# Routing in a two-layer diffusion kernel: seats of the first round from the prefix sums, gate work split, ranked weights behind the first gathers' index

## The reference

```python
aff = jax.nn.sigmoid((t @ router_w).astype(jnp.float32))
sel = aff + router_b.astype(jnp.float32)
...
_, idx = lax.top_k(jnp.where(in_group, sel, -jnp.inf), TOP_K)
wsel = jnp.take_along_axis(aff, idx, axis=-1)
wsel = wsel / jnp.sum(wsel, axis=-1, keepdims=True)
gates = jnp.sum(jax.nn.one_hot(idx, N_EXPERTS, dtype=jnp.float32) * wsel[..., None], axis=1)
a = jnp.einsum('nd,edf->nef', t, w1)
b = jnp.einsum('nd,edf->nef', t, w3)
hid = jax.nn.silu(a) * b * gates[..., None].astype(t.dtype)
return jnp.einsum('nef,efd->nd', hid, w2).reshape(B, L, D)
```

## Time and profile before

| what | value |
|---|---|
| median of 3 runs | 1009.19 us (1008.07 to 1012.16) |
| the profiled execution, its own time | 1012.8 us |
| its span, first to last instruction | 1010.7 us |
| PE busy | 896.8 us (89%) |
| DVE, ACT, POOL busy | 493.1 (49%), 250.9 (25%), 178.3 (18%) us |
| mean granted TensorE clock | 0.945 of full speed |
| moved by DMA | 213.74 MB |

### The profile page before, as it was taken

How to read it: one execution, slowest core, us unless ns; L and a number is a source line. 1 busy time by engine, 2 the same in 40 slices (tenths; PEclk the granted TensorE clock), 3 DMA queues, 4 the chain that set the end, 5 groups by cost and what they waited for, 6 DMA issues and landing times.

```text
span 1010.7 us, 12292 instructions
## 1 busy us (share of the span) xinstructions
PE 896.8 (89%) x4293; PEld 514.3 (51%) x4293; DVE 493.1 (49%) x1167; ACT 250.9 (25%) x606; POOL 178.3 (18%) x214
## 2 busy tenths in 40 slices
PE   2999989989979998969998989999998599689778
PEld 0685455655456544724443448747654463533223
DVE  1215763676879335533332371376577772422124
ACT  2202213535545112301111021221446240311000
POOL 1625220211000000320121101612112000121100
PEclk8899999999989998979998999999999799599899
DMA  9887222485700102778997591923584018869993
GB/s 373 264 240 222 83 84 84 170 317 209 290 16 2 42 0 89 284 284 295 387 420 304 207 339 76 252 83 97 182 320 153 0 57 323 328 232 398 418 400 136
DMA packets 69650, 213.74 MB, mean 211 GB/s; under 512 B 9690, under 2 KB 18178, under 8 KB 60372
## 3 DMA queue, kind: packets, MB, share of 16 engines
q1 hardware_dynamic: 58912, 187.81, 49.5%
q0 software_dynamic: 9504, 21.88, 6.9%
q10 hardware_dynamic: 1172, 3.24, 0.8%
HBM read 198.95 MB, written 21.31 MB: 218 GB/s over the span
## 4 chain that ended last, share of the span: by engine, by line
PE 74%; DVE 12%; issue 5%; DMA 4%; ACT 2%; POOL 2%; SPq 0%; DVEq 0%; ACTq 0%; POOLq 0%
PE bank L2014 14%; PE bank L1924 8%; PE bank L1720 8%; PE bank L1616 8%; PE bank L2038 7%; PE bank L1696 4%; PE bank L1870 3%; PE bank L1708 3%; PE bank L1803 3%; PE bank L1663 3%; DMA BRANCH<-in_w_mod 3%; PE bank L1891 2%; POOL ST L1249 2%; PE bank L1779 2%; PE bank L2071 1%
## 5 line engine op out<-in xcount | busy, mean ns | idle before, releaser
L2014 PE MATMUL bank<-RINGW,NA 128*64 128x512 f32 (+1 forms) x400 | 140.7, 619 | 20.6 <-issue 15.8
L1249 POOL TENSOR_TENSOR ST<-ST,RT 128x1 f32<-128x1 f32 (+4 forms) x46 | 52.0, 1132 | 409.7 <-DVE ST L2184 224.2
L1720 PE MATMUL bank<-RINGW,H 128*128 128x512 f32 (+4 forms) x384 | 120.7, 476 | 0.0
L2014 PEld LDWEIGHTS bank<-RINGW,NA 128*64 128x64 f32 (+1 forms) x400 | 51.3, 157 | 99.4 <-issue 99.4
L1720 PEld LDWEIGHTS bank<-RINGW,H 128*128 128x128 f32 x384 | 69.7, 193 | 49.1 <-issue 44.6
L1924 PE MATMUL bank<-RINGW,H 128*128 128x512 f32 x192 | 84.9, 603 | 0.1
L2801 DVE SCALAR_TENSOR_TENSOR BRANCH<-BRANCH,bank 128x256 f32<-128x256 f32 x20 | 8.4, 421 | 137.1 <-ACT BRANCH L1586 79.2
L1616 PE MATMUL bank<-IDENT,BRANCH 128*128 128x128 f32 (+1 forms) x271 | 40.9, 299 | 26.0 <-DVE BRANCH L2475 12.4
L1586 ACT ACTIVATE BRANCH<-bank 128x256 f32<-128x256 f32 x20 | 7.7, 384 | 214.0 <-PE bank L2014 214.0
L1924 PEld LDWEIGHTS bank<-RINGW,H 128*128 128x128 f32 x192 | 36.8, 193 | 45.4 <-issue 45.4
L1616 PEld LDWEIGHTS bank<-IDENT,BRANCH 128*128 128x128 f32 (+1 forms) x271 | 33.0, 148 | 45.7 <-issue 22.9
(11 more groups left out here) (354 smaller groups left out, 1525.9 us busy)
## 6 DMA issues: line engine op xcount, KB each, us to landing
RINGW<-in_moe_w SPq DMA_DIRECT2D x50, 1024.0 KB, 11.3
RINGW<-in_w_mod SPq DMA_DIRECT2D x23, 2048.0 KB, 8.2
WORK<-in_moe_w SPq DMA_DIRECT2D x14, 1024.0 KB, 12.8
W2R<-in_moe_w SPq DMA_DIRECT2D x12, 1024.0 KB, 12.3
PROJ<-in_moe_w SPq DMA_DIRECT2D x10, 1024.0 KB, 9.5
RINGW<-in_w_out SPq DMA_DIRECT2D x4, 2048.0 KB, 9.2
RINGW<-in_w_in SPq DMA_DIRECT2D x4, 1536.0 KB, 15.8
pairs<-NA POOLq DMA_DIRECT2D x12, 512.0 KB, 9.7
```

What stands on the lines that cost most here:

```text
L1249: pool.tensor_tensor(r[:, 0:w], m[:, 0:w], POOL_HALF[:, 0:w], ALU.pow).then_inc(rstd_ready, 1)
L1720: ins = pe.matmul(bank_of(s)[:, 0:nn], HT[:, kk, t * P:(t + 1) * P], wv[:, kk, off:off + nn], start=kk == 0, stop=kk == KD - 1)
L2014: ins = pe.matmul(bank_of(s)[seats, :], XGT[n % 2][:, kk, seats], w[:, kk, :], start=kk == 0, stop=kk == KD - 1)
```

## The change

- `sel` is made in one operation from the half-scaled tanh and a prepared bias (`BIASH`); `aff` is made behind `ASSIGN`.
- In `pfx`, DVE first makes the seats of round 0 straight from the prefix sums and the `SEND` rows from them (`IOTA` now counts from 1); the step `oh` is gone. Layer 0 needs one operation for the seats, layer 1 three.
- The gate work is split: up to the reciprocal it stays in `rT`, the other six operations stand in `pfx` behind `SEND` and ahead of `pick`.
- The list: `gdiff` goes ahead of `slots`, `gsel 0` goes behind `ab 0`.
- SP's load of the first ranked weights also waits for `index_ready`.

```diff
@@ make_schedule
-            if t == 3 and 0 in sq:
-                s += [("oh", l, 0)]
...
-        s += [("pfx", l, 1), ("oh", l, 1), ("gbc2", l)]
+        s += [("pfx", l, 1), ("gbc2", l)]
         s += [("xT", l, 0), ("tot", l)] if early else [("tot", l), ("xT", l, 0)]
-        s += [("slots", l), ("xg", l, 1), ("xg", l, 2), ("gdiff", l), ("gsel", l, 0), ("ab", l, 0)]
+        s += [("gdiff", l), ("slots", l), ("xg", l, 1), ("xg", l, 2), ("ab", l, 0), ("gsel", l, 0)]
@@ SP
                         sp.wait_ge(*full_of(("xT", p[1], 0, 1)))
                         sp.wait_ge(h2_stored, 16 * T)
+                        sp.wait_ge(index_ready, 1)
@@ DVE, gates
+                        link(dve.tensor_scalar(BIASH, bc_rb, 0.5, None, ALU.add))
@@ DVE, rT
-                    link(dve.tensor_scalar(aff, RT[:, 320 + 32 * s[2]:352 + 32 * s[2]], 0.5, 0.5, ALU.mult, ALU.add))
...
-                    link(dve.tensor_tensor(s3, a3, bc_rb.unsqueeze(1).broadcast_to([P, nt, 16]), ALU.add))
+                    half = RT[:, 320 + 32 * s[2]:352 + 32 * s[2]]
+                    link(dve.scalar_tensor_tensor(s3, half.rearrange("p (t e) -> p t e", e=16), 0.5,
+                                                  BIASH.unsqueeze(1).broadcast_to([P, nt, 16]), ALU.mult, ALU.add))
...
                     dve.wait_ge(assign_ready, pfx_n[("pfx",) + s[1:]])
+                    link(dve.tensor_scalar(aff, half, 0.5, 0.5, ALU.mult, ALU.add))
                     link(dve.tensor_tensor(gt, of_tiles(ASSIGN, t0), a3, ALU.mult))
                     link(dve.tensor_reduce(mx, gt, AX.X, ALU.add))
                     link(dve.reciprocal(mx, mx))
-                    link(dve.tensor_scalar(mx, mx, 0.5, None, ALU.mult))
-                    gv = GATEv[:, t0:t0 + 2, :]
-                    link(dve.tensor_tensor(gv, gt, bcast(mx, 16), ALU.mult))
-                    for c, oh in ((0, oh0), (1, oh1)):
-                        link(dve.tensor_tensor(prod, oh, gv, ALU.mult))
-                        link(dve.tensor_reduce(ENT[:, t0:t0 + 2, c, 1], prod, AX.X, ALU.add))
@@ DVE, pfx
                     bk = bank_of(s)
+                    pos, mine = of_tiles(bk, 0), of_tiles(ASSIGN, t0)
+                    sent_to = [SEAT[:, 2 * i:2 * i + 2] for i in (0, 1)]
+                    if l < DEPTH - 1:
+                        link(dve.tensor_tensor(sent_to[0], pos[:, :, 0], mine[:, :, 0], ALU.mult))
+                    else:
+                        half = N_E // 2
+                        dve.tensor_tensor(sent_to[0], pos[:, :, 0], mine[:, :, 0], ALU.mult)
+                        link(dve.scalar_tensor_tensor(sent_to[1], pos[:, :, half], float(P // 2), mine[:, :, half],
+                                                      ALU.add, ALU.mult))
+                        link(dve.tensor_tensor(sent_to[0], sent_to[0], sent_to[1], ALU.add))
+                    for i in (0, 1):
+                        ins = dve.tensor_scalar(SEND[0][t0 + i], IOTA[:, :], SEAT[:, i:i + 1], None, ALU.is_equal)
+                    ins.then_inc(send_ready, 1)
+                    mx = RT[:, 240:242]
+                    gt, prod = of_tiles(RT[:, 280:], 0), of_tiles(PROD, 0)
+                    link(dve.tensor_scalar(mx, mx, 0.5, None, ALU.mult))
+                    gv = GATEv[:, t0:t0 + 2, :]
+                    link(dve.tensor_tensor(gv, gt, bcast(mx, 16), ALU.mult))
+                    for c in (0, 1):
+                        link(dve.tensor_tensor(prod, of_tiles(OH[c], t0), gv, ALU.mult))
+                        link(dve.tensor_reduce(ENT[:, t0:t0 + 2, c, 1], prod, AX.X, ALU.add))
@@ DVE, iota
-                    dve.tensor_copy(IOTA[:, :], bank_of(s)[:, 0:P]).then_inc(iota_ready, 1)
+                    dve.tensor_scalar(IOTA[:, :], bank_of(s)[:, 0:P], 1.0, None, ALU.add).then_inc(iota_ready, 1)
@@ DVE, oh: the whole step is removed
-                        link(dve.tensor_scalar(SEAT[:, 2 * T * r + 2 * t0:2 * T * r + 2 * t0 + 4],
-                                               SLOTF[:, 2 * t0:2 * t0 + 4], -float(r), 1.0 / nr, ALU.add, ALU.mult))
...
-                            ins = dve.tensor_scalar(SEND[r][t], IOTA[:, :], seat(r, t, 0), None, ALU.is_equal)
...
-                            ins = dve.scalar_tensor_tensor(SEND[r][t], IOTA[:, :], seat(r, t, 1), SEND[r][t],
-                                                           ALU.is_equal, ALU.add)
```

More of the change, by code:

```diff
@@ L637, in build @@
         NOTOVER = ST[:, 250:251]
-        SEAT = ST[:, 136:136 + DIRECT * 2 * T]
+        SEAT = ST[:, 136:140]
+        BIASH = ST[:, 160:176]
         RSEAT = ST[:, 144:144 + 2 * 2 * T]
@@ L2740, in _ @@
                     tick(dve, free_of(s)[0])
[L2741 to L2746, removed]
-                        link(dve.tensor_scalar(SEAT[:, 2 * T * r + 2 * t0:2 * T * r + 2 * t0 + 4],
-                                               SLOTF[:, 2 * t0:2 * t0 + 4], -float(r), 1.0 / nr, ALU.add, ALU.mult))
-                    for r in range(DIRECT):
-                        for t in (t0, t0 + 1):
-                            ins = dve.tensor_scalar(SEND[r][t], IOTA[:, :], seat(r, t, 0), None, ALU.is_equal)
-                        link(ins)
-                        for t in (t0, t0 + 1):
-                            ins = dve.scalar_tensor_tensor(SEND[r][t], IOTA[:, :], seat(r, t, 1), SEND[r][t],
-                                                           ALU.is_equal, ALU.add)
-                        ins.then_inc(send_ready, 1)
                 elif k == "slots":
```

## The result

The changed kernel takes 1014.96 us in the median of 8 runs (1012.58 to 1018.19), the kernel before 1009.93 in the median of 8. The ratio is 1.0054 (95% interval 1.0034 to 1.0074): **5 us slower**. The forecast was 1006.3, with 999.5 to 1011 as the range. Of all runs in this document one, in the last experiment, was slow (1180 us, at a granted clock of 0.756); it is left out.

The account below looks back on a forecast made before the run. TensorE, busy for 89% of the span, was taken as the bound, so only its stalls matter. Layer 0's -3.4 and layer 1's +0.5 made -2.9 us: 1006.3 from the median of 1009.19, range 999.5 to 1011.

Parts of the forecast that it names:

- The gather of layer 1: Layer 1's first gather, issued 0.5 us ahead of the weights, takes 5.4 us and lands at 895.6: +0.5 us.
- rival B: Weights overtake layer 1's first gather at a lead below about half a microsecond: 9.8 us, +4.9 in layer 1; chance 0.10.
- the good bound of -1.3: Layer 1's best case: clock as before, `ab 0` ending at 891.8, gather alone: -1.3 us.
- The gather of layer 0: Layer 0's first gather takes 7.0 us instead of 9.73, landing at 438.3 against 441.70: -3.4 us for `xT 1`.
- the second load of a pair and the idle start: Layer 0: DMA engines idle at the gather's issue; from such a start a pair's second load took 7.0 us.
- The two slot-table loads at 2.1: Layer 0: with the weights held back, both slot-table loads take 2.1 us, the second no longer 4.72: -2.6 us.
- PE's wait for bank3: Layer 0, second group of `hT` transposes: PE waits 1.25 us for the later released prefix-sum bank; +1.2 us taken.
- `gbc2` straight into `xT 0`: Layer 1: SEND is ready earlier, so PE reaches `xT 0` without a stop, 1.6 us sooner.
- The price of the change in layer 0: Layer 0, ahead of the gather's issue: +1.2 us from the bank's later release, +0.7 from later scatters.
- rival C: Nothing left: layer 0's gather takes its 9.7 us again (-0.7), layer 1 loses 0.5: 1009 us; chance 0.17.
- A shift of the early rounds is carried to the end: Later stalls wait for weights whose loads PE's own progress starts, so a shift of the early rounds reaches the end.
- Rival A: Gathers share the queues and pass the weights, 4.5 us: layer 0 gains 5.9, layer 1 0.4; say 1002; chance 0.33.

Follow-up runs that it names:

- the last experiment: Changed kernel with signal in layer 0 only, bank of the prefix sums released ahead of the gate rows, layer 1's SEND rows behind the slot numbers: 1004.09 us, ratio 0.9930.
- before, tied to `ab 0`: Kernel before, with POOL issuing layer 1's first gather only when `ab 0` has ended: 1018.98 us, ratio 1.0104.
- changed, signal: Changed kernel; in layer 1 POOL signals by a tiny memset after issuing the first gather, and SP's weight loads wait for it: 1008.97 us, ratio 0.9986.
- changed, SEND late: Changed kernel with layer 1's two SEND rows put back behind the slot numbers: 1008.08 us, ratio 0.9977.
- changed, held: Changed kernel with SP in layer 1 waiting until the first gather has landed before issuing the weights behind `ab 0`: 1011.34 us, ratio 1.0004.
- the index wait alone: Kernel before with only SP's new wait: layer 0's first ranked weights issued once the first gathers' index is there; 1007.56 us, ratio 0.9980.

## Why the prediction was wrong

**The gather of layer 1 is the step that failed.** I put it at 5.4 us, "nearer to the first third, since it has the lead", with 7.4 as the bad end. It took 8.41. The mechanism stood among the rivals (B), with the place right and the deciding lead too small: "below about half a microsecond". The runs give the scale:

| first gather of layer 1 | weights behind it by, us | gather, us | layer 1's stretch, us |
|---|---|---|---|
| before, tied to `ab 0` | -0.86 | 8.26 | 116.53 |
| changed | 0.17 | 8.41 | 112.66 |
| changed, signal | 1.25 | 3.34 | 107.39 |
| changed, SEND late | 2.45 | 3.4 | 106.87 |
| changed, held | 3.33 | 3.27 | 109.69 |
| before | 4.29 | 3.3 | 107.02 |

The other traces agree: three more kernels with the weights at most 0.1 us behind have gathers of 8.27 to 8.45 us and stretches of 112.65 to 113.31, five more with 1.25 us or more have 3.3 us and 107.31 to 107.82. No first gather of layer 1 had a lead between 0.17 and 1.25 us; second and third gathers did, and took 8.8 us with 0.67, 6.9 with 0.91 and 4.6 with 1.08. So the turn lies near a microsecond and is not sharp. The packets say why: a gather's first packet came 1.7 us after its issue (in the kernel before and in the run with the signal), the weights' first only 1.0 to 1.1 us after theirs, so by an estimate from these two a lead of under some 0.7 us is none. POOL's own instruction for the gather lasts 1.06 of the 1.7 us. By the Trainium skill (Perfetto Trace Analysis, section DMA Instruction — SWDGE (GPSIMD)) the end of such an instruction in the profile is the moment when the last of its descriptors is written. The runs fit that: a lead shorter than 1.06 us (0.17) didn't help, one just longer (1.25) did; that this end is the exact border is not shown. My "lead" of 0.5 us was no lead. I had the 1.33 us of POOL's issue in my own text for layer 0 and didn't use it here. The 5.4 also doesn't fit the words beside it, since a third of the way from 3.3 to 7.0 is 4.5, and the good bound of -1.3 is -1.6 by its own numbers (895.1 to 890.23 + 3.3); neither slip matters beside 8.41.

**The clock behind it** I left out in layer 1: `xT 1` took 1.97 and `y 0` 5.00 us, at the lower level until about 899, against 1.1 and 3.65 at the higher one: 2.2 us. Counted from the prefix-sum row `xT 1` itself starts 4.1 later than in the kernel before (23.35 and 19.28). Together that is 6.3 at the end of `y 0`, of which 5.64 are left at the last wait for weights. So rival B's +4.9 was enough for the wait alone, and short because it left out the clock.

**The gather of layer 0** was mis-sized in the same way: 7.0 put, 9.27 measured (9.3 to 9.6 in the other traces where the weights come a third of a microsecond behind it). The two lines by which I chose it, the second load of a pair and the idle start, didn't apply: the weights were in the queues first (from 428 to 432, over three microseconds into the gather, only q1 has packets). So its -3.4 was -1.3 in this trace. Whether layer 0 gained at all is not shown: counted from the first `hT` row, `xT 1` starts at 39.79 in the trace of the kernel before but at 37.58 in that of the tied kernel, which has the same code there, and with the changed code at 38.52 here and at 39.57 to 39.63 in three other traces.

**What was right.** The two slot-table loads at 2.1 (1.95 measured); PE's wait for bank3, 1.25 put and 1.35 measured; in layer 1 `gbc2` straight into `xT 0`, the clock up before 881, and `ab 0` sooner: counted from the prefix-sum row the weights go out 2.5 us earlier (2.7 put), the gather 1.6 later (1.1 put). The price of the change in layer 0, 1.9 put, was that or more: the gather goes out 29.2 after the first `hT` row in this trace and 30.2 in five others with the same code, against 27.3 with the index wait alone. So in layer 0 the gain of the wait and the price of the seats and gate rows about cancel, as rival C had it, and layer 1's loss remains.

**"A shift of the early rounds is carried to the end"** was too simple. In the run that held the weights of layer 0 until the gather's landing, `xT 1` came some 4 us sooner and longer waits for weights took it back. Whether the start of the weights or the start of PE counts changes within layer 0.

Rival A (a gather passes quickly between the packets of the stream), to which I gave 0.33, falls: in no trace did a first gather that was issued within half a microsecond of the weights take under 8 us.

## What to carry to other kernels

Where a small transfer on the path and a large stream start close to one another, look at who reaches the queues first and not at who is issued first; a tiny operation behind the gather on its own engine, and a wait for that before the stream, made 8.4 us into 3.3 in layer 1 (in layer 0 9.3 into 4.1) and let the stream start one microsecond later against the gather (two in layer 0). An earlier result is a loss if the same event also starts the stream: making SEND later again won 5.8 us of layer 1's stretch. And before a chain is shortened, see whether the wait at its end is the length of a transfer under load; ordering the transfers was worth more than all the arithmetic that was moved.

## What the runs showed of the hardware that I had not expected

- About a microsecond of lead decides between a gather that is free of the stream and one that waits behind it: in layer 1 first gathers took 3.3 to 3.4 us with 1.25 us or more ahead of the weights and 8.3 to 8.5 with 0.17 or less; second ones with 0.91 and 1.08 lie between (6.9 and 4.6).
- A gather needs longer than a weight load from its issue to its first packet: 1.7 us (889.11 to 890.82 in the kernel before) against 1.0 (886.33 to 887.30 in the changed one), so it is overtaken by a load that is issued 0.17 us behind it.
- A gather that starts together with the 1 MB loads lands with the second of them: in the changed kernel's layer 1 at 894.57, the four loads at 891.1, 894.3, 897.5 and 900.8; in its layer 0 at 437.9, the first loads at 433.9 and 438.1.
- The small scatters are caught as well: 5.81 us instead of 2.1 for the last one, when the weights are issued 0.38 us behind it.
